# Attention scores of two key heads issued together in two 64-row halves of the array

## The reference, cut to what matters

```python
s = einsum('bqkgd,bskd->bkgqs', q, k) * (1 / sqrt(HEAD_DIM))   # HEAD_DIM 64
s = s + bias                                                   # window of +-128 tokens
p = softmax(concatenate([s, sink], axis=-1))[..., :-1]
a = einsum('bkgqs,bskd->bqkgd', p, v)
```

## Time and profile before

| what | value |
|---|---|
| median of 3 runs | 2216.11 us |
| span of the profiled execution | 2218.2 us |
| TensorE matmul busy | 2040.0 us (92%) |
| VectorE busy | 1584.9 us (71%) |
| ScalarE busy | 1197.9 us (54%) |
| mean granted TensorE clock | 0.934 |
| attention stage, layer 0 | 334 to 409 us |
| attention stage, layer 1 | 1419.5 to 1494.5 us |

### The profile page before, as it was taken

One profiled execution on the slowest core, in us unless ns is written; L12 is line 12 of the kernel. 1 busy time (PEld: TensorE's weight loads), 2 busy tenths in 40 slices (PEclk: granted clock), 3 DMA queues, 4 the chain that ended last, 5 costly groups with the idle time before them and its releaser, 6 DMA issues.

```text
span 2218.2 us, 28743 instructions
## 1 busy us (share of the span) xinstructions
PE 2040.0 (92%) x9618; PEld 1423.9 (64%) x9618; DVE 1584.9 (71%) x2210; ACT 1197.9 (54%) x1594; POOL 332.7 (15%) x142
## 2 busy tenths in 40 slices
PE   6979989895999999999899799899689999999994
PEld 1449878673666666666535598787556666666662
DVE  4452626646999999999663525465579999999993
ACT  2152126413878777787523311362357877778772
POOL 0021000003112122221000301000212212212110
PEclk9969989896999999999999798999789999999997
DMA  9730012136999999999794101102669999999984
GB/s 358 295 123 1 2 42 77 52 132 244 364 379 377 379 384 384 383 374 381 288 368 157 43 1 43 76 2 90 242 245 370 384 371 389 384 376 384 377 310 147
DMA packets 69290, 542.13 MB, mean 244 GB/s; under 512 B 6681, under 2 KB 9760, under 8 KB 44582
## 3 DMA queue, kind: packets, MB, share of 16 engines
q1 hardware_dynamic: 57222, 496.21, 57.3%
q0 software_dynamic: 11984, 44.83, 7.1%
HBM read 517.17 MB, written 26.48 MB: 245 GB/s over the span
## 4 chain that ended last, share of the span: by engine, by line
PE 89%; DVE 6%; issue 2%; DMA 1%; ACT 1%; SPq 1%; DVEq 0%; ACTq 0%; POOLq 0%
PE bank L969 48%; PE bank L778 10%; PE bank L661 6%; PE bank L924 5%; PE bank L857 2%; PE bank L878 2%; PE bank L839 1%; PE bank L819 1%; PE bank L680 1%; PE bank L717 1%; PE bank L986 1%; PE bank L979 1%; DVE arena_z L1393 1%; PE bank L867 1%; PE bank L897 1%
## 5 line engine op out<-in xcount | busy, mean ns | idle before, releaser
L1216 ACT ACTIVATE arena_h_r<-ring 128x1024 fp32r<-128x1024 f32 x480 | 504.7, 1061 | 162.2 <-PE bank L969 159.9
L1669 DVE TENSOR_TENSOR ring_r<-ring,arena_h_r 128x1024 fp32r<-128x1024 f32 x470 | 557.6, 1218 | 32.1 <-ACT arena_h_r L1216 25.2
L969 PE MATMUL bank<-arena_h_r,arena_u_r 128*80 128x512 f32 x1280 | 373.0, 398 | 4.6 <-DVE arena_u_r L1689 4.6
L1669 DVE TENSOR_TENSOR ring_r<-ring,arena_u_r 128x1024 fp32r<-128x1024 f32 x282 | 333.8, 1219 | 13.9 <-ACT arena_u_r L1216 8.2
L1216 ACT ACTIVATE arena_u_r<-ring 128x1024 fp32r<-128x1024 f32 x288 | 301.1, 1059 | 61.5 <-PE bank L969 61.5
L969 PE MATMUL bank<-ring_r,arena_u_r 128*80 128x512 f32 x1024 | 318.2, 392 | 0.0
L969 PEld LDWEIGHTS bank<-arena_h_r,arena_u_r 128*80 128x80 f32 x1280 | 188.1, 151 | 101.2 <-DVE arena_u_r L1689 6.3
L969 PE MATMUL bank<-arena_u_r 128*80 128x512 f32 x768 | 216.9, 391 | 0.0
L969 PEld LDWEIGHTS bank<-ring_r,arena_u_r 128*80 128x80 f32 x1024 | 152.0, 148 | 85.0 <-issue 1.1
L601 POOL DMA_INDIRECT x_res<-arena_z,iscat x32 | 88.5, 2765 | 643.3 <-DVE arena_z L1715 643.3
L969 PE MATMUL bank<-arena_h_r,arena_z_r 128*80 128x512 f32 x640 | 181.4, 398 | 3.7 <-DVE arena_z_r L1704 3.7
(11 more groups left out here) (258 smaller groups left out, 3066.8 us busy)
## 6 DMA issues: line engine op xcount, KB each, us to landing
ring<-in_exp_w SPq DMA_DIRECT2D x192, 2048.0 KB, 10.2
ring<-in_ada_w SPq DMA_DIRECT2D x24, 2048.0 KB, 16.3
ring<-in_w_in SPq DMA_DIRECT2D x4, 4096.0 KB, 15.1
ring<-in_w_out SPq DMA_DIRECT2D x2, 4096.0 KB, 13.1
arena_z<-x_res POOLq DMA_DIRECT2D x2, 2560.0 KB, 9.8
arena_z<-x_res POOLq DMA_DIRECT2D x10, 512.0 KB, 4.6
x_res<-arena_z POOLq DMA_DIRECT2D x10, 512.0 KB, 2.9
xn_dram<-arena_u POOLq DMA_DIRECT2D x10, 512.0 KB, 2.9
```

The lines of the kernel that those rows point to most:

```text
L969: mm = pe.matmul(bank[out + n][0:CAP, :], xs[:, c, :], w[:, n * 512:(n + 1) * 512], start=(c == 0 and part == 0), stop=(c == KC - 1 and pa ...
L1216: act.activation(high[c], slot[s][:, c, :], ACT.Copy).then_inc(high_ready, 1)
L1669: v.tensor_tensor(slot_r[s][:, c, :], slot[s][:, c, :], high[c], ALU.subtract).then_inc(low_ready, 1)
```

## The change

The query tile is copied whole into one buffer, with no zeros, in one ScalarE instruction. `att` goes through the heads as 0, 4, 1, 5, 2, 6, 3, 7, so that heads 2m and 2m+1 of the list have different key heads. TensorE issues the scores of two list entries at every even step: for each group of key columns first the matmul of rows 0 to 63 (key head 0, bank 4), then that of rows 64 to 127 (key head 1, bank 5), each with a contraction of 64. They wait until both reductions of the pair before are done (`sc_out` at least n, where it was n-1 for one head). The rest of a step stays as it was. POOL's two memsets and the semaphore `q_zero` are gone.

```diff
--- before.py
+++ after.py
@@ -183,7 +183,7 @@
         x0tok = hy[:, 6400:7680].rearrange("p (t n) -> p t n", t=NT)
 
 
-        qT = [a[:, 0:2560].rearrange("p (i t) -> p i t", i=4) for a in (arena_u, arena_h)]
+        qT = arena_u[:, 0:2560].rearrange("p (i t) -> p i t", i=4)
         kT = arena_u[:, 2560:3328]
         sbuf_s = [arena_u[:, 3328 + 512 * n:3840 + 512 * n] for n in range(2)]
         prob = [arena_u[:, 4352 + 512 * n:4864 + 512 * n] for n in range(2)]
@@ -290,7 +290,6 @@
         x0_mm = sem("x0_mm")
         x0_out = sem("x0_out")
         rope_done = sem("rope_done")
-        q_zero = sem("q_zero")
         qk_mm = sem("qk_mm")
         qk_a = sem("qk_a")
         sc_mm = sem("sc_mm")
@@ -400,7 +399,7 @@
             return h_high_z[:, a:b, 768 + (c - 4) * P:768 + (c - 3) * P]
 
 
-        att = [(b, h) for b in range(NT) for h in range(HEADS)]
+        att = [(b, g * 4 + i) for b in range(NT) for i in range(HEADS // KV) for g in range(KV)]
 
         def keys(b):
 
@@ -567,10 +566,6 @@
                         pool.wait_ge(w_hi, l * 16 + g * 4 + c // 2 + 1)
                         w, high_w = w_group(slot, g, c)
                         pool.tensor_tensor(w_group(slot_r, g, c)[0], w, high_w, ALU.subtract).then_inc(w_lo[0], 1)
-
-                hold(pool, used[1], l * ROUNDS + 3, const_in)
-                pool.memset(qT[0][HD:P, :, :], 0.0).then_inc(q_zero, 1)
-                pool.memset(qT[1][0:HD, :, :], 0.0).then_inc(q_zero, 1)
 
                 s, per, n = taken(proj_at("kv", NT - 1))
                 hold(pool, s, l * per + n, const_in)
@@ -845,19 +840,26 @@
                 mm.then_inc(inv_mm, 1)
 
 
+                def scores(n):
+
+                    at = 0
+                    for x, (col, w) in enumerate(keys(att[n][0])[0]):
+                        for g in range(KV):
+                            b, h = att[n + g]
+                            rows = slice(g * HD, (g + 1) * HD)
+                            mm = pe.matmul(bank[4 + g][:, at:at + w], qT[rows, h % 4, b * P:(b + 1) * P],
+                                           kT[rows, col:col + w], start=True, stop=True)
+                            if x == len(keys(b)[0]) - 1:
+                                mm.then_inc(sc_mm, 1)
+                        at += w
+
                 pe.wait_ge(yh_done, l + 1)
-                pe.wait_ge(q_zero, l * 2 + 2)
                 for n in range(len(att) + 3):
                     if n < len(att):
-                        b, h = att[n]
-                        if n >= 2:
-                            pe.wait_ge(sc_out, l * len(att) + n - 1)
-                        at = 0
-                        for col, w in keys(b)[0]:
-                            mm = pe.matmul(bank[4 + n % 2][:, at:at + w], qT[h // 4][:, h % 4, b * P:(b + 1) * P],
-                                           kT[:, col:col + w], start=True, stop=True)
-                            at += w
-                        mm.then_inc(sc_mm, 1)
+                        if n % 2 == 0:
+                            if n:
+                                pe.wait_ge(sc_out, l * len(att) + n)
+                            scores(n)
                     m = n - 2
                     if 0 <= m < len(att):
                         pe.wait_ge(p_done, l * len(att) + m + 1)
@@ -1132,10 +1134,8 @@
                     act.wait_ge(qk_mm, l * 7 + n + 1)
                     src = bank[3 + n % 3]
                     if n < 5:
-                        for g in range(KV):
-                            half = slice(g * HD, (g + 1) * HD)
-                            ins = act.activation(qT[g][half, :, n * P:(n + 1) * P],
-                                                 src[half, :].rearrange("p (i t) -> p i t", i=4), ACT.Copy)
+                        ins = act.activation(qT[:, :, n * P:(n + 1) * P], src[:, :].rearrange("p (i t) -> p i t", i=4),
+                                             ACT.Copy)
                     elif n == 5:
                         ins = act.activation(kT[:, 0:512], src[:, :], ACT.Copy)
                     else:
```

## The result

The changed kernel takes 2223.29 us, the median of 5 runs (2220.99 to 2229.26), the kernel before 2215.37 beside it. The ratio is 1.0032, 95% interval 1.0016 to 1.0047: slower by 7 us. Both intervals leave out 1, and the two ratios lie on either side of the 0.3% that the prediction took as the least that can be told from no change. The forecast was 2221, with a range of 2213 to 2237.

A forecast was written before the change was run, and what follows sets the result against it. The prediction took TensorE to bound the attention stage. Less score work but a loop through ScalarE's copy, with entering and the blocks, summed to +2.5 us per layer, +5 on the median 2216.11: 2221, range 2213 to 2237.

The forecast's parts named there:

- The bound now: Attention stage before the change: bound by TensorE, busy 71.5 of 75 us; 2.21 us per head, 4.42 for two.
- Part 1: Attention scores: two 64-row halves running at the same time take 14 us per layer of scores off TensorE.
- upper bound of concurrency: Scores of a pair: the first half is not delayed by the second, 0.88 us for 512 keys.
- serial rival: Scores: loads or matmuls of the two halves run one after the other; +16 us, 2232; chance 0.35, slower.
- Part 2: Attention: each change between 128-row and 64-row matmuls costs 0.20 us, 40 changes per layer; 0.26 if waiting for the modelled end.
- Part 3: TensorE's order in attention: values wait for ScalarE's copy behind the exponential; 4.47 us per pair against 4.42, TensorE's work 3.96.
- Block 4: Reduction 32 to the end: both reductions precede the next scores, with subtractions between; 12.35 us against 11.66, +0.7 per layer.
- Entering: Start of attention: scores 2 and 3 wait for reductions 0 and 1, +0.7 us per layer; block 0 adds +0.3.
- wrong altogether: Signs in attention: pairs below 4.2 us, no wait on L1174, or a granted clock falling in blocks 0 to 3.
- likeliest case: Attention: parallel halves, ScalarE's copy the new wait; 2217 to 2226 us; chance 0.50, split 0.3 no change, 0.2 slower.
- Part 4: Fewer query copies, no memsets: no gain; last copy ends at 313.4, the inverse transform waits for VectorE's product at 315.1.
- fast rival: Attention: TensorE stays the bound because ScalarE's copy is in time after all; -12.6 us, 2203.5; chance 0.07.

The follow-up runs named there:

- e2: Kernel before with ScalarE's copy moved ahead of the exponential of the same step; 2209.09 us, ratio 0.9970 to before.
- e8: Kernel before with 64-row scores one head at a time, plus an unread matmul in the other half beside each; 2228.96 us, ratio 1.0058.
- e1: Changed kernel with ScalarE's copy of transpose n-2 moved ahead of exponential n; 2206.01 us, ratio 0.9971 to before.
- e6: Changed kernel with ScalarE's copy ahead of the exponential and three unused 512-column matmuls at the attention entry; 2205.26 us, ratio 0.9957 to before.
- e5: Changed kernel with three unused 512-column matmuls filling idle time at the attention entry; 2219.71 us, ratio 1.0019 to before.
- e11: The same kernel as e6, run again; 2197.63 us, ratio 0.9912 to before.
- e3: Kernel before with one query buffer and 64-row scores, one head at a time in the old order; 2349.05 us, ratio 1.0602.
- e7: Changed kernel with all score matmuls of the first half issued before those of the second; 2229.52 us, ratio 1.0057 to before.
- e10: The changed kernel as it is, run again on another occasion; 2222.19 us, ratio 1.0024 to before.

## Why the prediction was right

- **The bound now.** TensorE in blocks 1 and 2, right: e2 leaves 4.42 per pair untouched. "A whole head's time to spare" for the copy was wrong at the entry and in narrow blocks; that didn't enter the sum for the change.
- **Part 1, parallel halves.** Right: 1.15 for twelve score instructions against 1.10 for six. The prediction took the upper bound of concurrency by a narrow margin, on an absence of evidence in rows 6. That was a choice and not a proof, and it came true; the serial rival has fallen. The Trainium skill's rule that tiles load and multiply in parallel (TensorEngine Tiling (Array Packing), section Tiling Modes) agrees with these rows.
- **Part 2, change of shape.** Right in kind, 0.20 was a third too much: e8 gives 0.15 on average, and not the 0.26 of an engine that waits for its end at each change. In the changed kernel the way from the first score to the reduction took 1.29 and not 1.24, so that the loop came out at 4.47 as forecast.
- **Part 3, the loop.** Right, and the centre of the case: 4.47 predicted and measured, idle time on L1174, 0.42 per pair; opened in e1, it goes and the time falls by 17 us. 35.6 for reductions 8 to 24 and 14.7 for block 3 came out to 0.1. The gain that the loop hid was larger than the 0.5 per pair of the sum: with the loop open, scores follow scores after 3.78 in a pair without a wait (e6), not 3.96.
- **Block 4** was given +0.7 and brought 0.0 in both profiled executions of the changed kernel (0.5 in layer 1 of e5, for a reason that is open): its pairs wait for VectorE's and ScalarE's queues in both kernels, and I had added the queue to the chain where the two overlap.
- **Entering** was given +1.0. Without a fall of the clock it is +0.94 (13.53 in e5).
- **What was missing** is the clock at the entry. It stood among the signs of being wrong, without a price and without a place. The sign came: the prediction calls a granted clock that falls in blocks 0 to 3 "wrong altogether", and it fell in block 0, while the loop itself was right. With e5 as the measure, structure is some 1.7 to 2.2 per layer, 4 in all, and the clock another 1 to 4 in the medians. Two errors, 1.4 too much in block 4 and nothing for the clock, partly cancel in the total of +5 against +5 to +7, so part of the close match is luck. Had the clock been priced, the likeliest case would have leaned to slower instead of giving it 0.2 against 0.3.
- **Part 4** has held as far as it shows: the last copy ends at 306.4, and TensorE's inverse transform starts at 311.9, released by VectorE's product. The memsets alone were not tried.
- The fast rival (2203.5) needed the loop open. Its 12.6 us were near the truth: e6's two stages are together 11.5 shorter than e2's, which has the same swap, and e11's ratio to before is clearly under e2's (0.9912, to 0.9925 at most, against 0.9970). The times of e1, e6 and e11 (2197.6 to 2206) hold more than the halves, since the swap alone brings the kernel before to 2209, and e1 loses most of the halves' gain to the clock.

## What to carry to other kernels

When a change cuts the work of the busiest engine and batches it, write down the loop that closes over one batch, through every engine and in each one's program order; if that loop is longer than the work that is left, the gain becomes waiting, and the cure may be two instructions swapped on an engine with time to spare. Try the same swap on the kernel before, or its own gain is booked on the change. Price the filling of the pipeline too: an entry that waits for two results in place of one idles TensorE where it idled already, and the clock may fall there. If matmuls of 64 rows stand in a dense stream, try to give both halves work: with one half alone in use for the scores, the whole stage ran at 1.2 GHz here.

## What the runs showed of the hardware

- Score matmuls of 64 rows with the other half idle, between 128-row transposes and value matmuls, came with a granted clock at 0.51 for 140 us, TensorE busy all along (e3); a matmul without use beside each, in the other half, brought it to 0.98 (e8).
- Two row halves load and multiply together, and they do so even when the whole of one stands ahead of the other in the program: the second sets in 0.32 us after the first, and both take 1.47 us (e7), against 1.15 where they are issued side by side.
- Going from 128 rows to 64, or back, costs 0.15 us per change on average in a dense stream (e8).
- At the entry of attention (idle 1.71 us, 0.93 of matmuls, idle 1.37) the granted clock fell to 1.2 GHz for 3.4 us in one layer and for 13.7 in the other of one execution, and for 13.7 in both of another (e10). With a second idle time of 0.19 (before), or with matmuls in most of the idle time (e5), it did not fall.
